# A decoder layer with gathered experts: V gathers interleaved earlier and in another ratio, and the first diagonals moved on ScalarE

## What is computed

```python
q = (h @ w_query).reshape(B, S, 8, 2, 128)
s = einsum('bshcd,hckd->bshck', q, sub_keys)      # 8 heads, 2 halves, 128 keys
top_s, top_i = top_k(s, 16)                       # 16 + 16 candidates, then the best 16 of 256 sums
eid = i1 * 128 + i2                               # 16 experts a head and token, of 16384
a = gelu(einsum('td,thkd->thk', hx, expert_u[e])) # 128 dots of 2048 a token
out = einsum('thk,thkd->td', gw * a, expert_v[e]) # weighted sum of 128 rows
```

## Time and profile before

| | us |
|---|---|
| median of 3 runs (1731.44 to 1732.49) | 1732.29 |
| the profiled execution: its time | 1736.38 |
| the profiled execution: span from first to last instruction | 1734.7 |
| busy: TensorE matmul | 1519.0 |
| busy: VectorE | 1339.1 |
| busy: GpSimd (issuing gathers) | 956.7 |
| busy: ScalarE | 411.8 |
| DMA, mean over the span | 355 GB/s |

### The profile page before, as it was taken

One profiled execution on the slowest core, in us unless ns is written; L12 is line 12 of the kernel. 1 busy time (PEld: TensorE's weight loads), 2 busy tenths in 40 slices (PEclk: granted clock), 3 DMA queues, 4 the chain that ended last, 5 costly groups with the idle time before them and its releaser, 6 DMA issues.

```text
span 1734.7 us, 17134 instructions
## 1 busy us (share of the span) xinstructions
PE 1519.0 (88%) x6242; PEld 946.7 (55%) x6242; DVE 1339.1 (77%) x1907; ACT 411.8 (24%) x907; POOL 956.7 (55%) x591
## 2 busy tenths in 40 slices
PE   9999999999979915887778888799999899999976
PEld 8988999988668812333223333355545554444432
DVE  6666656666796999777767878887867877888898
ACT  5665456564201212011000101020223311000000
POOL 3210000000364677887787676788888456768782
PEclk9999999999989956999999999999999889999998
DMA  9876443467699999999999999999999999999997
GB/s 322 280 266 219 122 147 122 130 203 250 263 381 412 371 425 426 408 425 426 425 426 423 418 420 416 425 414 421 422 423 425 350 421 375 415 404 419 416 427 306
DMA packets 159381, 615.40 MB, mean 355 GB/s; under 512 B 20915, under 2 KB 74255, under 8 KB 96703
## 3 DMA queue, kind: packets, MB, share of 16 engines
q0 software_dynamic: 79232, 485.32, 68.2%
q1 hardware_dynamic: 80064, 128.99, 20.8%
HBM read 683.42 MB, written 2.10 MB: 395 GB/s over the span
## 4 chain that ended last, share of the span: by engine, by line
PE 29%; POOL 23%; DMA 16%; DVE 15%; issue 14%; DVEq 2%; ACT 1%; POOLq 0%; SPq 0%; ACTq 0%
PE psum_all L594 14%; POOL v_slot L549 11%; DMA v_slot<-in_expert_v_dram,eid 10%; POOL u_slot L530 10%; DVE u_slot L1814 9%; DMA u_slot<-in_expert_u_dram,eid 5%; PE psum_all L734 4%; PE psum_all L991 3%; POOL v_slot L552 2%; PE psum_all L759 2%; PE psum_all L715 1%; DVE xh L1850 1%; PE psum_all L621 1%; PE psum_all L619 1%; DMA wq_ring<-in_w_query_dram 0%
## 5 line engine op out<-in xcount | busy, mean ns | idle before, releaser
L1814 DVE SCALAR_TENSOR_TENSOR u_slot<-u_slot,xh 128x2048 f32<-128x2048 f32 x256 | 578.2, 2288 | 135.7 <-DMA u_slot<-in_expert_u_dram,eid 133.6
L991 PE MATMUL psum_all<-v_slot,diag 128*128 128x512 f32 x1152 | 555.6, 634 | 141.2 <-DMA v_slot<-in_expert_v_dram,eid 94.1
L530 POOL DMA_INDIRECT u_slot<-in_expert_u_dram,eid x256 | 453.1, 1770 | 290.9 <-DVE u_slot L1814 118.4
L549 POOL DMA_INDIRECT v_slot<-in_expert_v_dram,eid x224 | 404.5, 1806 | 117.6 <-issue 69.9
L991 PEld LDWEIGHTS psum_all<-v_slot,diag 128*128 128x128 f32 x1152 | 223.2, 201 | 450.5 <-issue 249.9
L1850 DVE SCALAR_TENSOR_TENSOR xh<-v_slot,gate,xh 128x2048 f32<-128x2048 f32 x100 | 235.2, 2352 | 51.4 <-DMA v_slot<-in_expert_v_dram,eid 44.2
L1432 DVE TENSOR_TENSOR w_lo<-w_ring,w_hi 128x512 fp32r<-128x512 f32 x240 | 156.6, 688 | 78.3 <-ACT w_hi L1040 75.1
L594 PE MATMUL psum_all<-act_hi,w_hi 128*128 128x256 f32 x640 | 184.6, 289 | 1.7 <-DVE w_lo L1432 1.6
L594 PE MATMUL psum_all<-act_hi,w_lo 128*128 128x256 f32 x640 | 180.7, 282 | 0.0
L594 PE MATMUL psum_all<-act_lo,w_hi 128*128 128x256 f32 x640 | 180.6, 282 | 0.0
L1040 ACT ACTIVATE w_hi<-w_ring 128x512 fp32r<-128x512 f32 x240 | 139.4, 623 | 42.7 <-PE psum_all L594 42.0
(11 more groups left out here) (296 smaller groups left out, 1627.0 us busy)
## 6 DMA issues: line engine op xcount, KB each, us to landing
w_ring<-in_w_in_dram SPq DMA_DIRECT2D x88, 512.0 KB, 4.9
u_slot<-in_expert_v_dram SPq DMA_DIRECT2D x40, 1024.0 KB, 8.9
wo_ring<-in_w_out_dram SPq DMA_DIRECT2D x32, 512.0 KB, 4.9
wq_ring<-in_w_query_dram SPq DMA_DIRECT2D x32, 512.0 KB, 9.0
w_ring<-in_cmp_k_w_dram POOLq DMA_DIRECT2D x16, 512.0 KB, 5.7
w_ring<-in_cmp_v_w_dram POOLq DMA_DIRECT2D x16, 512.0 KB, 4.3
u_slot<-in_expert_u_dram,eid POOLq DMA_INDIRECT x256
v_slot<-in_expert_v_dram,eid POOLq DMA_INDIRECT x256
```

Of the source, the lines that this page charges most:

```text
L530: nc.gpsimd.indirect_dma_start(out=u_slot[m % RU][:, :], out_offset=None, in_=expert_u[0], in_offset=bass.IndirectOffsetOnAxis(ap=eid[:, n ...
L549: nc.gpsimd.indirect_dma_start(out=v_slot[m % RV][:, :], out_offset=None, in_=expert_v[0], in_offset=src, bounds_check=ROWS - 1, oob_is_er ...
L991: ins = nc.tensor.matmul(bank[(4 if n < PH else 0) + q][:, :], diag[:, n % 2, k, :], v_slot[m % RV][:, 512 * q:512 * q + 512], start=(m in ...
L1814: V.scalar_tensor_tensor(u_slot[m % RU][:, :], u_slot[m % RU][:, :], 1.0, xh[:, n // PH, :], ALU.mult, ALU.mult, accum_out=u_dot[:, n, k:k ...
```

## The change

POOL's order of gathers changes in three numbers. `AHEAD` goes from 4 to 3, so 48 U gathers are written ahead of the interleaved loop in place of 64. V 0 to 3 are sent after U 47 (before: after U 55). From V 4 on, 48 + 4 (m + 1) / 3 U gathers (whole numbers, rounded down) are sent ahead of V m in place of 64 + 5 (m + 1) / 4. At V 144 the U gathers that are left are sent in a row: now 11 from U 245, behind the one sent for V 144 by the formula; then 15 from U 241, likewise. On ScalarE the diagonals of unit 0 are made ahead of the exponential and the gelu of unit 3 in place of behind them. The same gathers, dots, picks and products are done.

```diff
-AHEAD = 4
+AHEAD = 3
...
         for m in range(TOPK * AHEAD):
             gather_u(m // TOPK, m % TOPK)
-            if m == TOPK * AHEAD - 9:
+            if m == TOPK * AHEAD - 1:
                 for k in range(EARLY_V):
                     gather_v(0, k)
         sent = TOPK * AHEAD
         for m in range(EARLY_V, TOPK * NU):
-            while sent < min(TOPK * NU, TOPK * AHEAD + (m + 1) * 5 // 4):
+            while sent < min(TOPK * NU, TOPK * AHEAD + (m + 1) * 4 // 3):
                 gather_u(sent // TOPK, sent % TOPK)
                 sent += 1
...
         act.wait_ge(S["eps2_ok"], 1)
+        diagonals(0)
         unit(3)
-        diagonals(0)
         diagonals(1)
         unit(4)
```

## The result

The changed kernel takes **1773.89 us** (median of 4 runs, 1769.67 to 1780.15) against 1732.39 for the kernel before on the same chip: ratio 1.023, 95% interval 1.0215 to 1.0245. It is 41.5 us slower. The forecast was 1747.5 with a range to 1757, so the sign was right and the size was not. The profiled execution took 1776.36 us with a span of 1774.6.

The account below looks back on a forecast made before the run. Bytes (DMA engines near full, 422 GB/s) were taken to set the time from 607 to 1344 us. The terms 0 + 0 + 12.2 + 3 = +15.2 us on 1732.29 gave 1747.5 us, range 1733 to 1757.

Parts of the forecast that it names:

- Parts 1 and 2: V 0 to 3 after U 47, about 606.8; diagonals of unit 0 earlier, first pick about 632: 0 us each.
- The dip rated at -1.7: Early DMA dip around 718 to 724 us (359 GB/s): might vanish if TensorE starts sooner, about -1.7 us; 0 taken.
- Part 3, which gather stalls and on what: At V 100, POOL waits for pick 93's slot, held by hot rows after dot 178; DMA idles 12.2 us.
- Part 3, the chain: From U 177 landing to V 100's bytes: 15.7 + 9.6 + 0.3 + 1.0 + 0.6 = 27.2 us.
- The gap's bounds (7.9 to 14.0 us): DMA idle before V 100: 7.9 us with a warm TensorE, 14.0 with the 2.76 us issue of U 42.
- The variant of 12.6 us: The DMA gap at V 100 with the skill's fixed 2.0 us per transfer set against 1.6 us: 12.6 us.
- Work in the queues behind U 177: Seven gathers queued behind U 177, V 97 to U 181, would keep DMA busy 15.0 of the 27.2 us.
- Afterwards the gap does not grow: After V 100: TensorE needs 9.0 us for two picks, DMA 10.0 us for their gathers, so no further loss.
- Rival (c): Remaining fifteen hot-row steps each lose a microsecond when TensorE's clock falls: 12 to 15 us more, about 1761; chance 0.12.
- Part 4: Last U gathers in a row, sixteen: four more dots at VectorE's 3.34 us, not 2.46; +3 us (2.2 to 3.5).
- Nor is it given back, since what follows is bound by bytes: After the V 100 gap: none of the 12.2 us comes back, as bytes set the time of what follows.
- The rule on the clock: Skill says ramp under 1%, giving warm 5.3 us, gap 7.9; prediction took cold 9.6 us from row at 1360.95.

Follow-up runs that it names:

- experiment 1: Changed kernel with the old formula, 64 + 5(m+1)/4, from V 4 on: 1736.55 us, 1.0013. Kernel before with only the early diagonals: 1733.47 us, 1.0001.
- experiment 5: Kernel before with no U gather beyond U 239 sent until V 144, so sixteen stand in a row: 1736.8 us, 1.0018.

## Why the prediction was off, step by step

**Parts 1 and 2 (0 us each): right within the noise of 2 us.** V 0 went at 603.5 and the first pick at 629.7, both as foretold (606.8 and 632) once the 3 us are taken off by which the query stage ran earlier in this execution; 607 to 1080 kept 422 GB/s. The dip rated at -1.7 brought nothing that runs can show. Early V with the old formula cost some 2 us (experiment 1), for which the prediction has no term.

**Part 3, which gather stalls and on what: right.** V 100, pick 93, the hot rows after dot 178, with POOL's wait put to L991, TensorE's 31.2 us put to the hot rows (30 said) and a clock of 0.50. The distance is the cause: by the number of U gathers ahead of V 100 (in the second line, by the same distance to the hot rows) the runs give

| U gathers ahead of V 100 | time over before |
|---|---|
| 182 (the changed kernel) | +2.3% (41.5 us) |
| 186, or 182 with the hot rows four dots earlier | +0.58%, +0.61% |
| 190 (56 as offset; the kernel before has 190 too) | +0.06%, its interval holds 0 |
| 198 (64 as offset) | +13.3% |

**Part 3, the chain: right.** 27.6 us measured, 27.2 summed. The gap's bounds (7.9 to 14.0 us) came from this chain alone. The variant of 12.6 us set the fixed cost of a whole transfer against the 1.6 us from POOL's issue to the first bytes, which is another stretch; in the trace it is about 1.3 us (1136.89 to 1138.2).

**Part 3, "Work in the queues behind U 177 ... that is 4 x 2.46 + 3 x 1.72 = 15.0 us": this step failed.** The row for bytes was right, and the slowest engine did run for 15.4 us after the landing (until about 1126). But the sum took sixteen engines for one queue. It credited the whole rate for as long as the last of them worked, while the share at work was 0.66 after 2 us, 0.21 after 6 and 0.06 after 12. Behind the landing lay 5.2 us of full rate, and the gap was 22.4 us (23.5 in the run that has this gap alone) in the place of 12.2: 11 us of the miss.

**Part 3, "Afterwards the gap does not grow": failed.** The sum compared two rates for a TensorE that is warm and never waits, 9.0 against 10.0 us for two picks. After a stall the queue is shallow, dots wait for their U gathers (11.04 us for the first after the gap), the hot rows come late, TensorE idles for 4 to 5 us and goes cold, and the next V waits again. The refilled queue took all of this away; kept shallow it costs 18 us in the end, some 25 us lost up to 1380 less the 7 given back in the row. Rival (c) came nearest, with 12 to 15 us from the later hot-row steps and a chance of 0.12; but it laid them to the clock, a microsecond a step, and what the steps lost was a wait for gathers.

**Part 4 (+3): the number alone right, and perhaps by luck; wrong in company.** Four more U gathers in the row cost 3.1 us in the kernel before, with waits that the prediction didn't have (experiment 5); four fewer (offset 56) gained nothing, and in the changed kernel the row gave back 7 us of the stalls instead of adding 3. The bytes of late gathers found room where VectorE had left the DMA engines idle. The sentence "Nor is it given back, since what follows is bound by bytes" was wrong for this stretch.

**The rule on the clock.** The Trainium skill (TensorE: Matmul & The Clock Gate, Part 1) had put the ramp at under 1% of a span; I let the row at 1360.95 decide. The runs side with both: the row's duration was right for the chain (3.64), and the one warmed start was worth 2 to 4 us of 1774, 0.1 to 0.2%, not clear of the noise.

Together: 23.5 for the first gap (12.2 foretold), some 25 for the later ones (0), some -7 for the row (+3): 41.5 us. The last two are read from windows of single executions. The range failed since the two terms that failed had no bounds: the queued work was set by count alone, the later stalls at zero.

## What to carry to other kernels

Two streams in one in-order queue, each of which frees what the other waits for, have a window of distances: here 8 gathers nearer than the kernel that works cost 2.3%, 8 farther 13%, and another order at the same distance gained nothing. Count the distance at each point where the streams are tied, from both sides, against the depth of the slots. For what a stall costs, take the slope with which the DMA rate falls from a trace, not the bytes outstanding over the full rate, and ask what refills the queue afterwards; while nothing did, the stall came back at following ties here, 38 us in 13 waits.

## What was not expected of the hardware

When no new gathers came, the rate didn't stay full to the end: 418, 279, 205, 90 and 25 GB/s at about 0, 2, 3, 6 and 12 us after the landing of U 177, the last at one sixteenth of the DMA share. With V gathers of 128 rows each, it stayed at 418 to 434 for nearly 10 us and was at 78 within 4 more.

How long POOL takes to issue a gather hangs on VectorE's dots. Of the 338 gathers that the changed kernel issued between 620 and 1400 us, 171 began outside a dot and took 0.94 to 1.31 us, 155 of them at most 1.08. The other 167 began while a dot ran, and all but three of them ended 0.80 to 0.89 us after that dot did, so that they took up to 3.12 us. The issue of V 100 above (1.01) had VectorE idle; that of V 116, from 1239.06 to 1242.18, met dot 202, from 1239.02 to 1241.31.
